# Two blocks of a hybrid transformer: where the sixteen gate-rank columns are loaded

## The reference

```python
for l in range(2):                                   # first block
    h = _rmsnorm(x, norm_g[l])
    (u_a, v_a, z_a, c_q, c_kv, k_r, z_b, q_c, k_c, v_c, g_c, z_c, gate_logits) = _split_cols(h @ w_in[l])
    y_a = _spatial_gating(u_a, v_a, z_a, ...)
    y_b = _mla(c_q, c_kv, k_r, z_b, ...)             # latent attention: c_q 256, c_kv 128, k_r 32 columns
    y_c = _gla(q_c, k_c, v_c, g_c, z_c, ...)         # gated linear attention; g_c is 16 columns
    gates = jax.nn.sigmoid(gate_logits + b_gate[l]).reshape(bn, s, N_BRANCH, d)
    x = x + (gates[:, :, 0] * (y_a @ w_branch[l, 0]) + ...) @ w_out[l]
# _gla: log_a = log_sigmoid(g_c @ w_gu + b_gu) / 16, chunks of 64 tokens, a state carried over 4 chunks
# second block: window attention, mLSTM and gated delta net side by side, then cross attention
# to a memory, then a feed-forward of 4096 with squared relu, then a norm
```

## Time and profile before

| | |
|---|---|
| runs | 1040.87, 1037.69, 1038.01 us; median 1038.01 |
| profiled execution | 1041.72 us, span of the core 1040.0 |
| PE busy | 1016.9 us, 98% of the span |
| DVE, ACT, POOL busy | 747.8 (72%), 571.0 (55%), 70.5 (7%) |
| mean granted PE clock | 0.99 of full speed |
| DMA | 160.57 MB, mean 154 GB/s |

### The profile page before, as it was taken

One profiled execution on the slowest core, in us unless ns is written; L12 is line 12 of the kernel. 1 busy time (PEld: TensorE's weight loads), 2 busy tenths in 40 slices (PEclk: granted clock), 3 DMA queues, 4 the chain that ended last, 5 costly groups with the idle time before them and its releaser, 6 DMA issues.

```text
span 1040.0 us, 21726 instructions
## 1 busy us (share of the span) xinstructions
PE 1016.9 (98%) x9135; PEld 934.5 (90%) x9135; DVE 747.8 (72%) x1188; ACT 571.0 (55%) x841; POOL 70.5 (7%) x177
## 2 busy tenths in 40 slices
PE   9999999999999999999999999889999999999997
PEld 8778999999977999999998998779899899998885
DVE  5879677788877966787889967756778566555445
ACT  5775575444666558444468674125345456575333
POOL 8600000000000000011140000000000000000000
PEclk9999999999999999999999998989999999999999
DMA  9656554455664545448787440001355355555652
GB/s 326 178 182 176 153 156 129 145 176 178 196 181 129 154 136 158 126 151 240 160 206 203 123 153 24 24 22 47 118 174 179 126 157 181 178 184 184 196 187 81
DMA packets 73553, 160.57 MB, mean 154 GB/s; under 512 B 6917, under 2 KB 16320, under 8 KB 73456
## 3 DMA queue, kind: packets, MB, share of 16 engines
q1 hardware_dynamic: 70304, 150.59, 46.8%
q0 software_dynamic: 2832, 8.06, 4.0%
q10 hardware_dynamic: 320, 0.53, 0.1%
HBM read 158.11 MB, written 1.05 MB: 153 GB/s over the span
## 4 chain that ended last, share of the span: by engine, by line
PE 86%; DVE 6%; ACT 3%; DMA 2%; issue 2%; ACTq 0%; POOL 0%; DVEq 0%; POOLq 0%
PE psum L470 23%; PE psum L472 22%; PE psum L471 22%; PE psum L883 2%; PE psum L1034 2%; DMA ring<-in_w_in 2%; PE psum L872 1%; DVE ring_lo L1388 1%; PE psum L724 1%; PE psum L702 1%; ACT ring_hi L2446 1%; DMA ring<-in_w_branch 1%; DVE arena L1574 1%; PE psum L1308 1%; PE psum L716 1%
## 5 line engine op out<-in xcount | busy, mean ns | idle before, releaser
L1388 DVE TENSOR_TENSOR ring_lo<-ring,ring_hi 128x1024 fp32r<-128x1024 f32 (+4 forms) x291 | 342.7, 1195 | 174.3 <-ACT ring_hi L2446 172.7
L2446 ACT ACTIVATE ring_hi<-ring 128x1024 fp32r<-128x1024 f32 (+4 forms) x291 | 297.7, 1034 | 268.9 <-PE psum L472 247.4
L470 PE MATMUL psum<-hT,ring_hi 128*128 128x256 f32 x904 | 258.5, 286 | 0.5 <-DVE hT L1748 0.5
L472 PE MATMUL psum<-hT,ring_lo 128*128 128x256 f32 x904 | 255.6, 283 | 0.0
L471 PE MATMUL psum<-hT,ring_hi 128*128 128x256 f32 x904 | 255.2, 282 | 0.0
L470 PEld LDWEIGHTS psum<-hT,ring_hi 128*128 128x128 f32 x904 | 172.4, 191 | 3.0 <-issue 2.4
L471 PEld LDWEIGHTS psum<-hT,ring_hi 128*128 128x128 f32 x904 | 172.4, 191 | 0.0
L472 PEld LDWEIGHTS psum<-hT,ring_lo 128*128 128x128 f32 x904 | 172.4, 191 | 0.0
L470 PE MATMUL psum<-ring_hi,hT 128*128 128x512 f32 (+4 forms) x416 | 156.0, 375 | 1.9 <-DVE ring_lo L1388 1.1
L472 PE MATMUL psum<-ring_hi,hT 128*128 128x512 f32 (+4 forms) x416 | 151.9, 365 | 0.0
L471 PE MATMUL psum<-ring_lo,hT 128*128 128x512 f32 (+4 forms) x416 | 151.6, 364 | 0.0
(11 more groups left out here) (461 smaller groups left out, 1353.5 us busy)
## 6 DMA issues: line engine op xcount, KB each, us to landing
ring<-in_w_in SPq DMA_DIRECT2D x104, 512.0 KB, 3.6
ring<-in_w_ff SPq DMA_DIRECT2D x64, 512.0 KB, 3.5
ring<-in_w_branch SPq DMA_DIRECT2D x24, 512.0 KB, 3.3
ring<-in_w_out SPq DMA_DIRECT2D x24, 512.0 KB, 3.5
ring<-in_w_in SPq DMA_DIRECT2D x24, 384.0 KB, 3.3
ring<-in_w_xkv SPq DMA_DIRECT2D x16, 512.0 KB, 3.8
ring<-in_w_in SPq DMA_DIRECT2D x8, 528.0 KB, 4.1
ring<-in_w_xq SPq DMA_DIRECT2D x8, 512.0 KB, 4.1
```

Source lines behind the costliest of these rows:

```text
L470: mm(b, lhs[0], rhs[0], start=start, stop=False, **how)
L472: return mm(b, lhs[1], rhs[0], start=False, stop=stop, **how)
L1388: V.tensor_tensor(chunk_view(ring_lo, RAW, c), chunk_view(ring, RAW, c), plain(chunk_view(ring_hi, RING_HI, c)), ALU.subtract).then_inc(ev ...
L2446: AC(chunk_view(ring_hi, RING_HI, c), chunk_view(ring, RAW, c), ACT.Copy).then_inc(ev("whi_ready"), 1)
```

## The change

Slot 0 becomes 432 wide: to the latent attention's 416 columns, each of its four chunks gets a second part with g_c's 16 columns, by a DMA of its own. ACT copies these 16 columns of each token tile to their place in `proj` before it copies the 416. Slot 6 is z_c alone, 512 columns in one piece. Line numbers behind the edits are 4 higher, in ACT's and SP's streams up to 7.

```diff
-SLOTS1 = [(COL_CQ, 416, 1), (COL_U, 512, 1), (COL_V, 512, 1), (COL_Z, 512, 1), (COL_ZB, 512, 1),
-          (COL_QC, 512, 1), (COL_GC, 528, 2), (COL_VC, 512, 1)]
+SLOTS1 = [(COL_CQ, 416 + GRANK, 1), (COL_U, 512, 1), (COL_V, 512, 1), (COL_Z, 512, 1), (COL_ZB, 512, 1),
+          (COL_QC, 512, 1), (COL_ZC, 512, 1), (COL_VC, 512, 1)]
...
         for l in range(DEPTH):
             for c0, n, _ in SLOTS1:
-                w_cols(A["w_in"][l], c0, n)
+                if c0 == COL_CQ:
+                    w_cols(A["w_in"][l], c0, n - GRANK)
+                    w_cols(A["w_in"][l], COL_GC, GRANK, True)
+                else:
+                    w_cols(A["w_in"][l], c0, n)
...
                     n //= parts
                     for t in range(T):
+                        if c0 == COL_CQ:
+                            n = 416
+                            af(AC(proj[:, t, COL_GC:COL_GC + GRANK], full(act, ("p1", l, i, t, 0))[:, n:n + GRANK], ACT.Copy, scale=rx[:, t:t + 1]))
                         for q in range(parts):
                             copy_out(("p1", l, i, t, q), proj[:, t, c0 + q * n:c0 + (q + 1) * n], n, scale=rx[:, t:t + 1])
```

## The result

| | before | the change |
|---|---|---|
| median of the runs (range, n) | 1038.98 us (1037.69 to 1040.87, 5) | 1051.12 us (1047.13 to 1051.51, 5) |
| profiled execution, span | 1041.72, 1040.0 | 1051.51, 1049.8 |
| ratio, 95% interval | | 1.0109, 1.0087 to 1.013 |

The change makes the kernel slower, by 11.3 us by the ratio. Run once more beside the experiments it gave 1048.88 us, ratio 1.0097 (1.0072 to 1.0122). The side was forecast, the size was not: 1044.3 was said, and the range ended at 1047.0.

What follows compares the result with a forecast made beforehand. PE was taken as the bound, busy 1016.9 of 1040.0 us. Start 1.2, layer 1's slot 0 0.35, slot 6 -1.3, gates(4) 3.13 and second block 2.9 summed to +6.3: 1044.3 us, range 1040.3 to 1047.0.

Steps and rivals of the forecast that it cites:

- Bank waits of the first block: At gates(4), PE waits for DVE to free the bank of gu: +1.57 us in layer 0, +1.56 in layer 1.
- What a wait costs: At gates(4), each wait costs PE its full length, 1.57 and 1.56 us, as nothing can slip past.
- Start, +1.2: Layer 0's start: four small DMAs 0.9 us plus two narrow ACT copies 0.3, with slot 0's 0.35 lying inside.
- upper bound of 2.7: Layer 0's start: highest price of the four small DMAs, 64 packets an engine at 42 ns, 2.7 us.
- Slot 6, -0.65 a layer: Slot 6: 48 matmuls of 512 columns take 11.30 us in place of 11.95 for 96 of 264.
- rival 4: Slot 6: number of matmuls rules, 0.124 us each, so it takes 6.0 us; 1033.7 us in all; chance 0.02.
- milder form of it: Slot 6: by the Trainium skill's sustained figures, from about 9.4 to 6.3 us, the change near 1038; no chance of its own.
- Slot 0, +0.35: Slot 0: 16 more columns on 48 matmuls add 0.35 us a layer, counted as it is in layer 1.
- Second block, +2.9: Second block: bank waits of 1.2 us at each of two window scores, 0.3 at L1160, 0.2 at first window transposes.
- rival 1: Both blocks: waits on banks are met in time, leaving +0.25 us, 1038.3 us; chance 0.10.
- rival 2: Only the first block's stalls count, the second block's are absorbed: +3.4 us, 1041.4 us; chance 0.16.
- Rival 3: Start: the small DMAs cost 2.7 us in place of 0.9, 1046.1 us in all; chance 0.10.

Runs made afterwards that it cites:

- runs with the wait filled: Idle matmuls in gates(4)'s wait: changed kernel, twelve, 1049.07 us; kernel before with bank counter starting at 4, twelve, 1048.53 us, and six, 1045.71 us.
- the rotation alone: Kernel before with its counter of banks starting at 4 in place of 0, nothing else changed: 1047.27 us, ratio 1.0074.
- ACT as the issuer: Changed kernel, bank counter moved on by two after slot 6, ACT instead of SP issuing layer 0's four small DMAs: 1042.69 and 1042.67 us.

## Why the prediction failed, step by step

- **Bank waits of the first block**: right to 0.01 us. Forecast +1.57 and +1.56, measured +1.57 in layer 0, 1.57 of the 3.10 in layer 1, and 1.57 in both when only that wait was put in.
- **What a wait costs**: the step that failed. I wrote "it is a full loss" and priced each stall by its length. In layer 1 the clock fell behind it in four of five profiles, 1.5 us more. That the idle time makes it fall is what the runs with the wait filled point to, none of three, on few profiles.
- **Start, +1.2**: the second step that failed. I priced the four small DMAs by what their packets take on the 16 engines, 0.9 us. That time I had about right: in the packed trace of the changed kernel the packets of 64 B took 11 ns each, 0.7 us for the 64 of an engine, where I had 15 ns. The wrong step was to take that time for all that the start loses. It is late by 2.08 and 1.56 us in the two profiles of the changed kernel, by 0.09 to 4.27 in all six with these DMAs, and by the times they cost 4.8 us alone in the kernel before, above the upper bound of 2.7. I followed the delay only through the weights to 38.28: the chunk that ACT took at 25.48 is taken at 26.74, near the 26.4 that I said. The small rows that SP issues behind the weights, for which PE now waits at L688 (19.40 us before, at L684, where it did not wait), I did not follow; SP issues the first of them at 8.06 in place of 5.32. But with ACT issuing the DMAs the small rows are nearly on time and most of the loss stays. So SP's order is not shown to be all of it, and what carries the rest is open.
- **Slot 6, -0.65 a layer**: measured -0.50 and -0.49, 11.47 us for its 48 matmuls (88.98 to 100.45) where I had 11.3; the chunk's low part, which I left out as "the like of it", takes the rest. The openings of qkT behind it, which I costed at nothing, take back 0.19 and 0.15. The net is -0.31 and -0.34. The columns, not the instruction count, rule: rival 4 is out. So is the milder form of it that stands behind the rivals; its time, by my own sum, should have read about 1039, not 1038.
- **Slot 0, +0.35**: 0.29 in layer 1.
- **Second block, +2.9**: the waits at the window scores are 1.17 and 1.23 as forecast (1.2 each), L1160's 0.3 too, L876 has 0.9 in place of 0.5. In the profile of the rotation alone PE is late by 4.34 at the end of the first block and by 5.68 at the end of all, only 1.3 more, while the clock stood at one half for 10.2 us there against 17.1 in the profile of before; so the single waits are shown, but their sum can't be read there. By the times, 7.7 for all the waits less 3.4 and 4.1 for the wait at gates(4) alone leave 4.3 and 3.6 us for the second block, where I had 2.9; the intervals are too wide to call that a difference.
- **Rivals**: 1 and 2 fall with the rotation alone, +7.7 (5.6 to 9.7), where rival 1 has none of the waits and rival 2 those of the first block, which cost 3.4 and 4.1 alone. Rival 3, the small DMAs at their upper bound, was right in kind, but its bound was none, and its 1046.1 was too low as well.

By terms, from the times: rotation 7.7 where I had 6.0, start 4.8 where I had 1.2, slots about -0.4 where I had -0.95. The sum is 12.1, against 11.3 measured and 6.3 forecast. The rotation's interval, 5.6 to 9.7, takes in my 6.0. From the change's own pair of profiles: at the end of the first block PE is 6.39 late where my terms give 3.4, of which the clock is 1.5, the start 0.9 and the slots 0.6. The other 2 of the 5 us that are missing lie behind it, in the second block, and no profile places them.

By the Trainium skill ("DMA: Bandwidth & Descriptors", "Specifications"), transfers under 512 B are not at line rate. The packed trace agrees: 64 B in 11 ns are 5.8 GB/s an engine, 512 B in 27 ns are 19. The same page of the Trainium skill, section "Bandwidth", puts a packet at about 10.5 ns, and the 11 ns of the trace agree. But the estimate of 0.67 us that I worked out from it counts the packets' own time alone, and that is not what the start lost: rows of 512 B cost 2.2 us and rows of 64 B 4.8, and 2.6 us over the 56 packets an engine by which they differ would be 46 ns each.

## What to carry to other kernels

Where banks are handed out in rotation, taking two fewer in one place changes the previous tenant of every later opening: list tenants before and after, and if some slip, add the difference back to the counter (here one line was worth 7 us). Price an idle stretch of PE not only by its length but also by what it does to the clock behind it. Here that was 1.5 us more in layer 1, in four of five profiles. And small transfers in a start that is limited by DMA can cost several times their packets' own time: follow the delay to everything that is issued behind them, down to the last row that someone waits for, and measure a version without them.

## What the hardware showed that I had not expected

- The granted clock fell to one half for 3.4 us behind a wait of 1.5 us that followed small products, in four of five profiles at 435 to 437 us and never behind the same wait at 180 us; it also fell behind a wait of 3.5 us at 23 us. What sets the two places of gates(4) apart is open.
- Four DMAs of 256 rows of 64 B at a DMA share of 1.05 cost 4.8 us, the same bytes in 32 rows of 512 B 2.2, though the packets of 64 B took only 11 ns each, 0.7 us an engine. In single profiles the start of the 64 B form was late by 0.1 to 4.3.
- Medians of kernels with the same bank waits and starts that look alike still differ by 2 to 3 us (ACT as the issuer); the waits named "issue" at the inverse levels (L1034 and L883, with their later numbers) add up to 4.4 us before, 6.2 in the change, and 4.9 and 6.7 with ACT as the issuer, and I can't attribute them.
